# Two-layer encoder step with routed experts: the last rows gathered beside the expert loop end three pairs before the loop does

## The chip, the cores and the metric

The kernel runs on one core of a Trainium2 chip. The metric is the device time of one execution in microseconds (us). The core has five engines with queues of their own: TensorE (PE, matmuls), VectorE (DVE), ScalarE (ACT), GpSimd (POOL) and SyncE (SP), which here only issues transfers. Transfers that SP, ACT and POOL issue share 16 DMA engines.

## The reference

The program takes 512 new frames of one stream and 64 of another (576 tokens, 1024 numbers each) through two layers. Layer 0 mixes tokens with a chunked gMLP, layer 1 with windowed attention; each is followed by the expert step below, and a final norm ends the program. The expert step is where the change lies:

```
def peer_ffn(xn, w_q, sub_keys, exp_u, exp_v):
    q = (xb @ w_q).reshape(blk, PEER_HEADS, 2, D_HALF)
    sc = jnp.einsum('thpd,hpnd->thpn', q, sub_keys)
    ... # per token and head: the best 16 of 16384 experts, idx, with softmax gates
    act = jax.nn.gelu(jnp.einsum('thkd,td->thk', exp_u[idx], xb))
    w = (gate * act)
    return jnp.einsum('thk,thkd->td', w, exp_v[idx])
```

So every token needs, for 8 heads times 16 chosen experts, a dot product with a row of `exp_u` and a weighted sum of rows of `exp_v`.

## The kernel before

The tokens are split in two groups, and each group computes the expert step in its own way, at the same time.

**Dense group ("d", 256 tokens).** All 16384 experts are computed, 256 at a time: 64 "pairs" i = 0..63. For pair i, PE computes scores (`expert_scores`, L725, from `U`), ACT applies GELU (L1106), PE builds a matrix of gates from one-hot factors that DVE makes (`one_hot`, L1634 to L1645, `build`, L712), DVE multiplies gates and scores (`gate_product(l, i)`, L1656, written to `a`), and PE adds the pair's share to the output (`expert_sums`, L738, from `a` and `V`). Scores run 16 pairs (`RING`) and gates 17 pairs (`LEAD`) ahead of the sums. Therefore the last 16 pairs (i = 48..63) have sums and products only. `V` has two buffers: SP loads `V` of pair i + 2 (1 MiB, L451) when sums i are done. `a` has two buffers too: product i waits for sums i - 2. After sums 62, PE adds the residual `hx` with 16 matmuls (L779) and then does sums 63; ACT squares the eight results (L931), PE sums the squares (L541), and DVE turns the sum into the scale of the norm (`variance`, L1406, first instruction of `gathered_to_h` that computes).

**Gathered group ("g", 320 tokens).** Its chosen experts' rows are fetched. One step s (0..319, `NSTEP`) is one indirect DMA on POOL (L1325) that fetches 128 rows of 2048 numbers (1 MiB) into one of six slots (`SLOTS`, tiles `gata`, `gatb`). DVE multiplies and reduces against the tokens (`dot_x`, L1665), ACT makes the weight in two instructions (`weight`, L1112 and L1114), DVE adds the weighted rows to `acc` (`axpy`, L1673). `gathered(l, s)` is dot s and then axpy s - 1. The gather of step s waits for axpy s - 6. Below, a "row step" is one such s.

**Who sets the order.** Each engine runs its own list in order, and the lists are written by hand. The function `steps(l, i)` says which row steps DVE and ACT do in pair i; it takes the numbers from `step0`. On DVE, pair i of the last 16 is: product i + 1, then the row steps of pair i. The row steps thus stand between two products on one engine. Before the loop 57 (layer 0) and 58 (layer 1) row steps are done at fixed places; pairs 0..47 have 4 or 5 each. ACT does its two weight instructions per row step in the same order; in pair 63 it put the last ones between the squares.

PE's own list is not touched by the change, and neither are POOL's and SP's lists; what moves on them follows from waits.

Of the kernel before, what the change touches and what calls it, by code (L numbers as in the profile page):

```python
# [14 lines left out]
DT = D // P  # L15
# [7 lines left out]
NPAIR = NK // 2  # L23
# [14 lines left out]
RING, RING0 = 16, 9  # L38
# [116 lines left out]
def program(nc, xT, ckT, cv, gains, lin, uvd, uvg0, uvg1, skT, wsT, bs, sinks, dist, ident_c, iota_a, scaled_c, rank_c,  # L155
# [5 lines left out]
    with ExitStack() as ctx:  # L161
# [147 lines left out]

        def step0(l, i):  # L310

            n, last = NPAIR - RING, NPAIR
            if i <= n:
                return EARLY[l] + i * BUSY // 2
            rest = NSTEP - EARLY[l] - n * BUSY // 2
            return NSTEP - rest * max(last - i, 0) // (last - n)
# [28 lines left out]
        def steps(l, i):  # L345

            return range(step0(l, i), step0(l, i + 1))
# [28 lines left out]
        def dense_sum(d):  # L376

            return bank[4 + d // 2][:, TD * (d % 2):TD * (d % 2) + TD]
# [546 lines left out]
        def _(act):  # L925
            def square(name, src, dt):

                k, cols = NORM[name], COLS[name[-1]]
                if dt >= 2:
                    act.wait_ge(sq_used, (DT - 1) * k + dt - 1)  # L930
                act.activation(g[:, dt % 2, cols], src, ACT.Square).then_inc(sq_done, 1)  # L931
# [141 lines left out]
            def weights_at(l, place):  # L1073

                for s in early(l, place):
                    weight(l, s)

            def gates_high(l, c):
                b = 4 + c % 2
                act.wait_ge(full[b], BASE[f"gt{l}"][b] + 1)  # L1080
                act.activation(gh[:, TCO[c]:TCO[c] + TCS[c]], bank[b][:, 0:TCS[c]], ACT.Copy,
                               scale=GS).then_inc(gh_done, 1)

            def gate_exp(l, n):

                c = ORDER[n]
                act.wait_ge(sub_done, NTC * l + n + 1)
                act.activation(ex[0:TCS[c]], ex[0:TCS[c]], ACT.Exp).then_inc(exp_done, 1)

            def to_w(l, m):  # L1090

                b, c = 2 + m % 2, m // (TD // TB)
                act.wait_ge(full[b], BASE[f"bld{l}"][b] + m // 2 + 1)
                if m == 0:
                    act.wait_ge(h_out, 16 * (l + 1))
                if c >= 1:
                    act.wait_ge(a_done, NPAIR * l + m - PER + 1)
                act.activation(gate_block(c, m % PER), bank[b][:, :].rearrange("p (t j e) -> p j e t", t=TB, e=2),
                               ACT.Copy, scale=1.0 / GS).then_inc(free[b], 1)

            def gelu(l, i):

                act.wait_ge(full[i % 2], BASE[f"peer{l}"][i % 2] + i // 2 + 1)
                if i >= RING:
                    act.wait_ge(a_done, NPAIR * l + i - RING + 1)
                act.activation(scored(i), bank[i % 2][:, :], ACT.Gelu_apprx_tanh).then_inc(free[i % 2], 1)  # L1106

            def weight(l, s):

                k = s % 8  # L1110
                act.wait_ge(dot_done, NSTEP * l + s + 1)
                act.activation(act8[:, k:k + 1], dot[:, k:k + 1], ACT.Gelu_apprx_tanh).then_inc(act_done, 1)  # L1112
                act.wait_ge(act_done, NSTEP * l + s + 1)
                act.activation(wgt[:, k:k + 1], act8[:, k:k + 1], ACT.Copy, scale=gateg[:, s:s + 1])\  # L1114
                    .then_inc(wgt_done, 1)

            def experts(l):
                n = 0
                for i in range(2 if l else 3, NTC):
                    for k in range(FIRST[l][i] - 1):  # L1120
                        gelu(l, n + k)
                    n += FIRST[l][i]
                    gate_exp(l, i)
                    gelu(l, n - 1)
                    weights_at(l, f"sel{i}")
                    gelu(l, n)
                    n += 1
                for c in DC:
                    gates_high(l, c)
                for i in range(n, RING0 - 1):  # L1130
                    gelu(l, i)
                n = max(n, RING0 - 1)
                weights_at(l, "hot0")
                for m in range(1, LEAD):
                    weights_at(l, f"hot{m}")
                    to_w(l, m - 1)
                    if m % 2 == 1 and n + m // 2 < RING - 1:
                        gelu(l, n + m // 2)
                for i in range(NPAIR):
                    todo = steps(l, i)  # L1140
                    if i == NPAIR - 1:
                        act.wait_ge(full[7], BASE[f"peer{l}"][7] + 1)
                        for dt in range(DT):
                            square(f"n{3 + 2 * l}d", dense_sum(dt), dt)
                            if dt % 2 == 1 and dt // 2 < len(todo):
                                weight(l, todo[dt // 2])
                        todo = todo[DT // 2:]
                    for s in todo[:HEAD]:
                        weight(l, s)
                    if i + LEAD - 1 < NBLD:  # L1150
                        to_w(l, i + LEAD - 1)
                    if i <= NPAIR - RING:
                        gelu(l, i + RING - 1)
                    for s in todo[HEAD:]:
                        weight(l, s)
# [19 lines left out]
            gmlp("d")  # L1175
            selection(0, "d", 2)
            experts(0)

            def squares_of_sums(l):
# [113 lines left out]
            squares_of_h("n4d", "od")  # L1293
            selection(1, "d", 1)
            experts(1)
            squares_of_sums(1)

# [617 lines left out]
```

## Time and profile before

| | |
|---|---|
| median of 3 runs | 3138.45 us (3132.91 to 3144.28) |
| the profiled execution | 3128.67 us, of which the span is 3126.9 us |
| PE matmul busy | 2918.8 us, 93% of the span |
| DVE busy | 2452.2 us, 78% |
| ACT, POOL busy | 793.5 us (25%), 1023.0 us (33%) |
| transfers | 1042.97 MB, mean 334 GB/s |
| mean granted TensorE clock | 0.959 |

A busy PE is not PE at its peak, and a share over the span mixes stages with different limits. So the stage to read is the last 16 pairs of each expert loop: about 1351 to 1529 us in layer 0 and 2937 to 3107 us in layer 1.

### The profile page before, as it was taken

To read this page: it belongs to the slowest core of one execution; us is meant where nothing else is said; L and a number is where in the kernel's file an instruction comes from. 1 tells how busy PE (TensorE), PEld (TensorE's weight loads), DVE (VectorE), ACT (ScalarE), POOL (GpSimd) and SP (SyncE) were. 2 spreads that over 40 slices of the span, in tenths; PEclk is the share of its full clock that TensorE was granted. 3 is DMA by queue.
4 is the path that set the end of the run, shared out by engine and by line. 5 is a ranking of instruction groups with operands and counts; after the bars stand their busy time and mean duration, and the time that the engine had idled before them with its cause. 6 is when DMAs were issued, how large, how long until landed. Compare 5 with 4: busy or idle time off the path is not lost. (4 is left out here: it accounts for less than half of the span.)

```text
span 3126.9 us, 46521 instructions
## 1 busy us (share of the span) xinstructions
PE 2918.8 (93%) x17342; PEld 2556.9 (82%) x17342; DVE 2452.2 (78%) x5319; ACT 793.5 (25%) x2326; POOL 1023.0 (33%) x840
## 2 busy tenths in 40 slices
PE   8898999999999999987888978989999999999977
PEld 7797789888888888876667957879888888888865
DVE  2377899988888888887644777998888888888868
ACT  5332222211121211211354352222111111212112
POOL 5533222322233333333365321222223333333322
PEclk9898999999999999999999979989999999999989
DMA  5327778899999999999622258778999999999997
GB/s 186 102 89 289 306 300 319 349 421 422 421 422 422 416 422 419 418 410 422 230 92 75 93 190 319 283 293 312 422 422 421 422 421 418 421 415 416 413 421 289
DMA packets 159964, 1042.97 MB, mean 334 GB/s; under 512 B 18480, under 2 KB 23920, under 8 KB 44096
## 3 DMA queue, kind: packets, MB, share of 16 engines
q0 software_dynamic: 92160, 671.13, 52.6%
q1 hardware_dynamic: 63648, 357.59, 29.4%
q10 hardware_dynamic: 4000, 12.36, 1.0%
q8 instruction: 74, 1.21, 0.2%
q14 instruction: 82, 0.67, 0.1%
HBM read 1033.28 MB, written 7.86 MB: 333 GB/s over the span
## 5 line engine op out<-in xcount | busy, mean ns | idle before, releaser
L738 PE MATMUL bank<-a,V 128*128 128x256 f32 x4096 | 927.9, 386 | 62.6 <-DVE a L1656 51.2
L725 PE MATMUL bank<-xd,U 128*128 128x256 f32 x4096 | 939.0, 389 | 3.7 <-DMA U<-uvd 3.7
L738 PEld LDWEIGHTS bank<-a,V 128*128 128x128 f32 x4096 | 791.2, 194 | 182.6 <-issue 55.7
L1325 POOL DMA_INDIRECT gata<-uvg,idxg x428 | 496.3, 1159 | 1257.2 <-DVE acc L1673 1197.1
L725 PEld LDWEIGHTS bank<-xd,U 128*128 128x128 f32 x4096 | 789.3, 195 | 112.0 <-DMA U<-uvd 4.7
L1665 DVE CUSTOM_DVE_ANT_0 gata<-gata,xrow 128x1024 f32<-128x1024 f32 x428 | 522.2, 1220 | 222.2 <-DMA gata<-uvg,idxg 220.3
L1112 ACT ACTIVATE act<-dot 128x1 f32<-128x1 f32 x640 | 129.5, 202 | 1672.8 <-DVE dot L1665 1672.7
L1673 DVE SCALAR_TENSOR_TENSOR acc<-gata,wgt,acc 128x1024 f32<-128x1024 f32 x428 | 547.7, 1280 | 2.5 <-ACT wgt L1114 2.3
L1325 POOL DMA_INDIRECT gatb<-uvg,idxg x212 | 251.0, 1184 | 522.6 <-DVE acc L1673 513.1
L1665 DVE CUSTOM_DVE_ANT_0 gatb<-gatb,xrow 128x1024 f32<-128x1024 f32 x212 | 258.7, 1220 | 107.7 <-DMA gatb<-uvg,idxg 106.7
L712 PEld LDWEIGHTS bank<-B,oneA 128*128 128x128 f16 x4096 | 279.3, 150 | 29.9 <-issue 12.8
L712 PE MATMUL bank<-B,oneA 128*128 128x32 f16 x4096 | 283.2, 246 | 14.3 <-DVE oneA L1639 7.2
L1673 DVE SCALAR_TENSOR_TENSOR acc<-gatb,wgt,acc 128x1024 f32<-128x1024 f32 x212 | 271.2, 1279 | 1.9 <-ACT wgt L1114 1.9
L524 PE MATMUL bank<-xd,raw 128*128 128x256 f32 x1088 | 251.0, 388 | 7.5 <-DVE xd L1424 7.1
L524 PEld LDWEIGHTS bank<-xd,raw 128*128 128x128 f32 x1088 | 208.5, 195 | 37.3 <-issue 9.0
L511 PE MATMUL bank<-xh,wh 128*128 128x320 f32 x608 | 200.4, 330 | 29.3 <-POOL xl L418 25.3
L1114 ACT ACTIVATE wgt<-act,gateg 128x1 f32<-128x1 f32 x640 | 188.8, 295 | 20.8
L512 PE MATMUL bank<-xl,wh 128*128 128x320 f32 x608 | 190.9, 314 | 0.0
L513 PE MATMUL bank<-xh,wl 128*128 128x320 f32 x608 | 190.7, 314 | 0.0
L1639 DVE TENSOR_TENSOR oneA<-iotaA,i 128x1024 f16<-128x1024 f16 x256 | 169.9, 703 | 0.0
L511 PEld LDWEIGHTS bank<-xh,wh 128*128 128x128 f32 x608 | 116.9, 192 | 40.4 <-issue 33.7
L1359 POOL TENSOR_TENSOR wl<-raw,wh 128x1024 fp32r<-128x1024 f32 x48 | 115.8, 2414 | 100.6 <-ACT wh L941 100.5
(198 smaller groups left out, 2441.3 us busy)
## 6 DMA issues: line engine op xcount, KB each, us to landing
U<-uvd SPq DMA_DIRECT2D x128, 1024.0 KB
V<-uvd SPq DMA_DIRECT2D x128, 1024.0 KB, 9.0
raw<-lin SPq DMA_DIRECT2D x152, 512.0 KB, 3.6
gata<-uvg,idxg POOLq DMA_INDIRECT x428, 14.7
hsp<-h ACTq DMA_DIRECT2D x2, 2304.0 KB, 14.8
hx<-hsp SPq DMA_DIRECT2D x2, 2304.0 KB, 16.9
gatb<-uvg,idxg POOLq DMA_INDIRECT x212, 14.7
sk_g<-skT ACTq DMA_DIRECT2D x2, 1024.0 KB, 4.9
```

Source lines behind the costliest of these rows:

```text
L511: pe.matmul(out, whi, xh[:, k, :], start=(k == 0), stop=False)
L512: pe.matmul(out, whi, xl[:, k, :], start=False, stop=False)
L513: mm = pe.matmul(out, wlo, xh[:, k, :], start=False, stop=(k == DT - 1))
L524: mm = pe.matmul(bank[s][:, 0:TD], raw[:, s, P * k:P * k + P], x[:, k, :], start=(k == 0), stop=(k == DT - 1))
L712: mm = pe.matmul(bank[2 + s][:, CHUNK * t:CHUNK * (t + 1)], oneA[:, s, t // TG, :, t % TG], B[:, s, part, :, t], start=(t == 0 and part == ...
L725: mm = pe.matmul(bank[s][:, TD * t:TD * t + TD], U[:, s, o:o + P], xd[:, k, :], start=(t == 0 and k == 0), stop=(k == DT - 1), skip_group_ ...
L738: mm = pe.matmul(bank[b][:, TD * (d % 2):TD * (d % 2) + TD], V[:, s, o:o + P], a[:, s, TD * k:TD * k + TD], start=(first and k == 0 and d ...
L1114: act.activation(wgt[:, k:k + 1], act8[:, k:k + 1], ACT.Copy, scale=gateg[:, s:s + 1])\
L1325: pool.indirect_dma_start(row(l, s), None, uvg[l], bass.IndirectOffsetOnAxis(idxg[:, s:s + 1], 0)).then_inc(g_in[s % SLOTS], 16)
L1639: ins = dve.tensor_tensor(oneA[:, s, u], iotaA[:, :, :], i1[:, None, t + TG * u:t + TG * u + TG].broadcast_to([P, P, TG]), ALU.is_equal)
L1665: dve.tensor_tensor_reduce(u, u, xrow[:, min(s // P, 2), :], 1.0, 0.0, ALU.mult, ALU.add, dot[:, s % 8:s % 8 + 1]).then_inc(dot_done, 1)
L1673: dve.scalar_tensor_tensor(out=acc[:, n, :], in0=row(l, s)[:, D:RD], scalar=wgt[:, s % 8:s % 8 + 1], in1=acc[:, n, :], op0=ALU.mult, op1=A ...
```

## The change

`step0(l, i)` gives the first row step of pair i. For the last 16 pairs it divides what remains (47 row steps in layer 0, 46 in layer 1) evenly. Before, it divided by 16, now by 13, so that pairs 61, 62 and 63 get none. Row steps of pairs 48..63:

| | before | after |
|---|---|---|
| layer 0 | 3 in each, 2 in pair 63 | 4 4 3 4 4 3 4 3 4 4 3 4 3 0 0 0 |
| layer 1 | 3 in each, 2 in pairs 55 and 63 | 4 4 3 4 3 4 3 4 3 4 3 4 3 0 0 0 |

In pair 63 ACT no longer has weights to put between the squares, and the code for that goes.

```
@@ -309,7 +309,7 @@
         def step0(l, i):
 
-            n, last = NPAIR - RING, NPAIR
+            n, last = NPAIR - RING, NPAIR - 3
             if i <= n:
                 return EARLY[l] + i * BUSY // 2
             rest = NSTEP - EARLY[l] - n * BUSY // 2
@@ -1142,9 +1142,7 @@
                         act.wait_ge(full[7], BASE[f"peer{l}"][7] + 1)
                         for dt in range(DT):
                             square(f"n{3 + 2 * l}d", dense_sum(dt), dt)
-                            if dt % 2 == 1 and dt // 2 < len(todo):
-                                weight(l, todo[dt // 2])
-                        todo = todo[DT // 2:]
+                            assert not todo
                     for s in todo[:HEAD]:
                         weight(l, s)
```

The change shifts the line numbers behind it by two: L1656, L1665 and L1673 of before are L1654, L1663 and L1671 of after.

DVE's list near the end of layer 1's loop, before, from product 63 (the first row) through the row steps of pair 62 (315 to 317) to those of pair 63:

```order
L1656 TENSOR_TENSOR a_86<-gr_74,Wr_73 128x512
L1665 ISA gata_80,dot_66<-gata_80,xrow_58 128x1024
L1665 ISA dot_66 128x1
L1673 SCALAR_TENSOR_TENSOR acc_77<-gata_80,wgt_68,acc_77 128x1024
L1665 ISA gatb_81,dot_66<-gatb_81,xrow_58 128x1024
L1665 ISA dot_66 128x1
L1673 SCALAR_TENSOR_TENSOR acc_77<-gata_80,wgt_68,acc_77 128x1024
L1665 ISA gatb_81,dot_66<-gatb_81,xrow_58 128x1024
L1665 ISA dot_66 128x1
L1673 SCALAR_TENSOR_TENSOR acc_77<-gatb_81,wgt_68,acc_77 128x1024
L1665 ISA gata_80,dot_66<-gata_80,xrow_58 128x1024
L1665 ISA dot_66 128x1
```

After, from row step 317 of the 320 (its dot is the first row) to the first instruction of the norm:

```order
L1663 ISA gatb_81,dot_66<-gatb_81,xrow_58 128x1024
L1663 ISA dot_66 128x1
L1671 SCALAR_TENSOR_TENSOR acc_77<-gatb_81,wgt_68,acc_77 128x1024
L1663 ISA gata_80,dot_66<-gata_80,xrow_58 128x1024
L1663 ISA dot_66 128x1
L1671 SCALAR_TENSOR_TENSOR acc_77<-gatb_81,wgt_68,acc_77 128x1024
L1663 ISA gata_80,dot_66<-gata_80,xrow_58 128x1024
L1663 ISA dot_66 128x1
L1671 SCALAR_TENSOR_TENSOR acc_77<-gata_80,wgt_68,acc_77 128x1024
L1654 TENSOR_TENSOR a_86<-gr_74,Wr_73 128x512 x2
L1671 SCALAR_TENSOR_TENSOR acc_77<-gata_80,wgt_68,acc_77 128x1024
L1404 TENSOR_SCALAR rstd_61<-bank3 128x256
```

Before, product 63 has five row steps behind it (315 to 319), and product 62 has eight (312 to 319), three of them ahead of product 63. After, products 62 and 63 stand next to each other (the row with x2) behind dot 319 and axpy 318; only the last axpy is behind them.

ACT's list at the same place, before:

```order
L931 ACTIVATE g<-bank 128x256 x2
L1112 ACTIVATE act_67<-dot 128x1
L1114 ACTIVATE wgt<-act_67,gateg 128x1
L931 ACTIVATE g<-bank 128x256 x2
L1112 ACTIVATE act_67<-dot 128x1
L1114 ACTIVATE wgt<-act_67,gateg 128x1
L931 ACTIVATE g<-bank 128x256 x4
L937 ACT_TABLE_LOAD
```

and after:

```order
L1112 ACTIVATE act_67<-dot 128x1
L1114 ACTIVATE wgt<-act_67,gateg 128x1
L1112 ACTIVATE act_67<-dot 128x1
L1114 ACTIVATE wgt<-act_67,gateg 128x1
L931 ACTIVATE g<-bank 128x256 x8
L937 ACT_TABLE_LOAD
```

The two last weights move ahead of the eight squares.

## Rows read from the trace of the kernel before

**Rows 1.** The page: the span in 40 equal slices.
```profile
DMA  5327778899999999999622258778999999999997
GB/s 186 102 89 289 306 300 319 349 421 422 421 422 422 416 422 419 418 410 422 230 92 75 93 190 319 283 293 312 422 422 421 422 421 418 421 415 416 413 421 289
```

**Rows 2.** The page: groups of the row steps, and what transfers take to land.
```profile
L1665 DVE CUSTOM_DVE_ANT_0 gata<-gata,xrow 128x1024 f32<-128x1024 f32 x428 | 522.2, 1220 | 222.2 <-DMA gata<-uvg,idxg 220.3
...
L1673 DVE SCALAR_TENSOR_TENSOR acc<-gata,wgt,acc 128x1024 f32<-128x1024 f32 x428 | 547.7, 1280 | 2.5 <-ACT wgt L1114 2.3
...
V<-uvd SPq DMA_DIRECT2D x128, 1024.0 KB, 9.0
...
gata<-uvg,idxg POOLq DMA_INDIRECT x428, 14.7
...
hx<-hsp SPq DMA_DIRECT2D x2, 2304.0 KB, 16.9
```

**Rows 3.** Windows of layer 1's last 16 pairs (last two columns: DMA share, GB/s).
```profile
2970.00:3000.00 30.00, 22.82 (x93) 18.77 (x92) 22.29 (x30) 4.14 (x17) 9.93 (x9) 0.89 1.01 421
...
3080.00:3090.00 10.00, 7.93 (x29) 6.54 (x29) 7.77 (x11) 1.49 (x6) 3.76 (x3) 0.83 1.02 422
3090.00:3100.00 10.00, 10.00 (x48) 8.81 (x47) 10.00 (x14) 1.99 (x8) 1.14 (x1) 1.00 0.72 290
```

**Rows 4.** Timeline of DVE, layer 1: products 49, 62, 63; dot 319; norm.
```profile
2947.30 0.68 DVE L1656 TENSOR_TENSOR a<-gr,Wr 128x512 f32<-128x512 f32 x1
...
3081.45 0.69 DVE L1656 TENSOR_TENSOR a<-gr,Wr 128x512 f32<-128x512 f32 x1
...
3091.40 0.68 DVE L1656 TENSOR_TENSOR a<-gr,Wr 128x512 f32<-128x512 f32 x1
...
3101.38 1.22 DVE L1665 CUSTOM_DVE_ANT_0 gata<-gata,xrow 128x1024 f32<-128x1024 f32 x1
...
3106.77 0.43 DVE L1406 TENSOR_SCALAR rstd<-bank 128x256 f32<-128x256 f32 x1 [1.47 <-PE bank L541]
```

**Rows 5.** Timeline of PE, layer 1: sums 61, sums 62, residual, sums 63, norm.
```profile
3071.38 8.83 PE L738 MATMUL bank<-a,V 128*128 128x256 f32 x32 [3.73 <-DVE a L1656]
3082.29 8.83 PE L738 MATMUL bank<-a,V 128*128 128x256 f32 x32 [2.07 <-DVE a L1656]
3090.95 3.62 PE L779 MATMUL bank<-hx,ident 128*128 128x256 f32 x16
3094.41 7.07 PE L738 MATMUL bank<-a,V 128*128 128x256 f32 x32
3102.04 4.62 PE L541 MATMUL bank<-g,ones 128*128 128x256 f32 x16 [0.56 <-ACT g L931]
```

**Rows 6.** Timeline of DVE, layer 0: products 49, 62, 63; dot 319; norm.
```profile
1359.78 0.69 DVE L1656 TENSOR_TENSOR a<-gr,Wr 128x512 f32<-128x512 f32 x1
...
1497.63 0.69 DVE L1656 TENSOR_TENSOR a<-gr,Wr 128x512 f32<-128x512 f32 x1
...
1506.61 0.68 DVE L1656 TENSOR_TENSOR a<-gr,Wr 128x512 f32<-128x512 f32 x1
...
1522.65 1.23 DVE L1665 CUSTOM_DVE_ANT_0 gata<-gata,xrow 128x1024 f32<-128x1024 f32 x1 [0.47 <-DMA gata<-uvg,idxg]
...
1528.67 0.42 DVE L1406 TENSOR_SCALAR rstd<-bank 128x256 f32<-128x256 f32 x1 [2.19 <-PE bank L541]
```

**Rows 7.** Timeline of PE, layer 0: sums 62 and sums 63.
```profile
1498.46 7.14 PE L738 MATMUL bank<-a,V 128*128 128x256 f32 x32 [1.11 <-DVE a L1656]
...
1508.90 7.07 PE L738 MATMUL bank<-a,V 128*128 128x256 f32 x32
```

**Rows 8.** Timeline of SP and a window, end of layer 0's loop.
```profile
1474.87 22.84 SPq L451 DMA_DIRECT2D V<-uvd  x3
1497.88 1.96 SPq L435 DMA_DIRECT2D raw<-lin  x4
...
1510.00:1520.00 10.00, 7.07 (x32) 5.60 (x30) 6.03 (x8) 1.82 (x7) 0.00 (x0) 0.97 0.89 364
```

More of the change, by code:

```diff
@@ L310, in step0 @@
         def step0(l, i):
-            n, last = NPAIR - RING, NPAIR
+            n, last = NPAIR - RING, NPAIR - 3
             if i <= n:
@@ L1144, in experts @@
                             square(f"n{3 + 2 * l}d", dense_sum(dt), dt)
-                            if dt % 2 == 1 and dt // 2 < len(todo):
-                                weight(l, todo[dt // 2])
-                        todo = todo[DT // 2:]
+                        assert not todo
                     for s in todo[:HEAD]:
```

## The prediction

> **What bounds the kernel now.** I read the 40 slices of the page first, then the windows of the last 16 pairs, then the timelines of DVE and PE at the end of both loops. The slices show long stretches at 410 to 422 GB/s with the DMA engines full [rows 1]. In the last 16 pairs the reader is to see the same: DMA share 1.01, 421 GB/s, while PE is busy for 22.8 of 30 us and DVE for 22.3 [rows 3]. So here neither engine is full, and the transfers set the pace: in layer 1 from product 49 to product 62 pass 3081.45 - 2947.30 = 134.15 us [rows 4]. In that time DVE does the row steps of pairs 48 to 60, which are 38 (12 pairs of 3 and one of 2). With 13 loads of V (V50 to V62) and the one load of hx (2.25 MiB [rows 2]) that is 53.25 MiB, 2.52 us per MiB or 416 GB/s. DVE's own work on a row step is shorter, 1.22 + 1.28 us less an overlap of about 0.1 [rows 2], some 2.4 us.
>
> The end is a different matter, and there the order on DVE counts. PE waits for product 61 (3.73 us) and for product 62 (2.07 us); then it runs sums 62, the residual, sums 63 and the norm's sums without a hole to speak of [rows 5]. From the start of product 62 to the norm's first DVE instruction at 3106.77 is one unbroken chain of 25.3 us [rows 4]. Eight row steps (312 to 319: three of pair 61, three of pair 62, two of pair 63) stand behind product 62 on DVE and run beside that chain. They end at 3101.38 + 1.22 and two axpys, about 3105, before it does. In layer 0 the chain would end alone at about 1497.63 + 24 us = 1522; the norm starts only at 1528.67 [rows 6], because dot 319 begins at 1522.65 and ACT's last weights stand between the squares. There the rows decide, by some 7 us. They are late because SP issues four tiles of the next weights (raw, 2 MiB together) right behind V63 at 1497.88 [rows 8].
>
> **The change, part by part.**
>
> Removed and added instructions: none on DVE, PE, POOL or SP; ACT has the same 640 pairs of weight instructions. Everything is order, and bytes stay the same.
>
> *Where the rows end up.* Product 62 had eight row steps behind it and now stands behind all of them, but for axpy 319. So it comes when all 320 gathers have landed. I work that time out in two ways for layer 1.
> (a) By pace: from product 49 the remaining 46 row steps, 13 loads of V and hx are 61.25 MiB. Some 3 MiB come off: at the end of the measured stretch six gathers were issued and about half moved, and now none is left. 58.25 x 2.52 = 146.8 us, which gives 2947.3 + 146.8 = 3094.1.
> (b) By the end of all transfers: the window 3090 to 3100 moves 290 GB/s, 2.9 MB, which at 421 GB/s last until 3096.9 [rows 3]. Of this, V63 now goes behind the rows (it waits for sums 61), 2.5 us; the last row has landed at 3094.4, a straggling landing may cost 0 to 3 us, and dot 319 and axpy 318 take 2.4: 3096.8 to 3099.8.
> I take 3097.5, nearer to (b), which rests on the end itself. Product 62 therefore moves by 3097.5 - 3081.45 = +16.0 us.
> The same for layer 0: (a) 1359.78 + (47 + 13 + 2.25 - 3) x 2.52 = 1509.1; (b) window 1510 to 1520 with 364 GB/s ends at about 1518.6 [rows 8], less V63 and the four raw tiles (3 MiB, 7.6 us) is 1511.0, plus 2.4 and a straggling landing of 0 to 4 (dot 319 began 4 us after 1518.6): 1513.4 to 1517.4. I take 1514.5.
>
> *What follows it.* The chain behind product 62 has nothing beside it that can be taken off: product 0.7, sums 62 7.1 to 8.8, residual 3.5, sums 63 7.1, squares and their sums 5.3 [rows 5, 7], which is 23.6 to 25.3 us. ACT's two weights (about 0.5 us each) go from between the squares. In layer 1 that gives nothing: PE's 16 norm matmuls last 4.62 us back to back [rows 5]. In layer 0 they no longer wait for a late row, and this gain is in the numbers below.
> Layer 1: 3097.5 + 25.3 = 3122.8 against 3106.77, +16.0 us.
> Layer 0: 1514.5 + 24.5 = 1539.0 against 1528.67, +10.3 us.
> What comes behind the norm (transposes of acc, the next layer, the stores) is unchanged and moves as a block; axpy 319 waits for product 63 and so for sums 61, but is done long before PE asks for acc.
>
> *What is costed at nothing, and its cover.* The pairs 48 to 60 get longer (from 134.15 / 13 = 10.3 us to about 11.5 us each), so PE waits more in each. That is off the path, since PE needs 7.1 to 8.8 us a pair. V63 is issued when sums 61 end. Product 61 is three row steps ahead of product 62, 8 to 10 us, so sums 61 end at about 3096 to 3099, and V63 lands 9.0 us later [rows 2], at 3105 to 3108. Sums 63 ask for it at 3097.5 + 0.8 + 8.8 + 3.5 = 3110.6. The cover is some 3 us. In layer 0 the raw tiles are issued behind V63: 3 MiB in 7.6 us from about 1514, done by 1524, asked for at 1527. If this cover is gone the price is the lateness itself, 1 to 4 us per layer.
>
> *The sum:* 10.3 + 16.0 = +26.3, with rounding +27 us. Against the profiled execution 3128.67 + 27 = 3155.7 us. That execution lies 9.8 us under the median of the runs, so against the median it is 3138.45 + 27 = **3165 us**, 0.86% slower.
>
> **A rule beside the row.** The row shows 421 GB/s for whole stretches [rows 3]. The Trainium skill, "DMA: Bandwidth & Descriptors", section "Where 436 GB/s comes from", gives about 358 GB/s per core as the bound for transfers from HBM and 435 GB/s as that of the fabric. At 358 GB/s (an estimate from that page) 58.25 MiB would take 170.6 us and product 62 would come at 3118 rather than near 3095; the trace is above this bound by 63 GB/s, and the measurement decides.
>
> **The rivals.**
>
> 1. *Faster: the gathers had room, and denser rows fill it.* If the pace of before was set by the thin list (3 rows per pair, each slot refilled only after its axpy) and not by bytes, then 3.5 rows per pair run at DVE's floor: 46 x 2.4 + 13 x 0.6 = 118 us, product 62 at 3065.5 in layer 1, 16 us earlier than before; in layer 0 1359.8 + 120.6 + 24.5 = 1504.9, 24 us earlier. That gives 3138.45 - 40 = 3098 us. For it: DVE is idle for a quarter of the stretch, waiting for gathers. Against it: DMA share 1.01 [rows 3]. It decides when a MiB takes under 134.15 / 58.25 = 2.30 us (455 GB/s) in layer 1, which no window shows. Chance 0.03. The skill's page named above has the fabric's 435 GB/s as ceiling, so by its rule this rival is shut as well.
>
> 2. *About the same.* The landing of rows gets shorter where fewer loads of V compete, and the pace comes to 2.40 us per MiB (437 GB/s): product 62 at 2947.3 + 139.8 = 3087.1 (+5.7) and at 1502.0 in layer 0, whose norm is then at 1526.5 (-2.2). In sum +3.5, 3142 us. For it speaks that single slices and windows reach 422 to 424; against it that none reaches 437. Chance 0.08.
>
> 3. *Slower still.* V63 or the clock adds to the tail. Product 62 comes as late as 3100.5 and 1518, V63 is 2 to 4 us late, and sums 62 and 63 run partly at 1.2 GHz: sums 62 took 8.83 us after an idle stretch of 2.07 us and 7.14 after one of 1.11 [rows 5, 7], with a granted clock down to 0.83 in that window [rows 3]. Longer idle time in front could raise both sums to about 2 x 7.1 = 14.2 us, up to 5 and 7 us more. Sum +38 to +50, 3176 to 3188 us. Against it: the last three rows drain at 2.4 to 3.2 us, so that product 62 comes about when sums 61 end, and PE has no wait there. Chance 0.07. The skill, "TensorE: Matmul & The Clock Gate", section "HAM oscillation — how this bites in real kernels", says that an engine that waits for transfers in every round begins every round at the low clock; by it, sums 62 would be at 8.8 rather than 7.1 us, which is the value that I took for layer 1.
>
> That the change doesn't do what it says is excluded by the lists of the engines: the two products stand side by side at the end.
>
> **How the numbers follow.** My own case has 0.82. Its bounds: product 62 from 3094 to 3100 with a chain of 23.6 to 25.3 us, +10.8 to +19; layer 0 from 1509 to 1518 likewise, +4 to +14.6. Together +15 to +34, 3153 to 3172 us. To leave out no more than 2 in 10 the range is stretched a little towards rivals 2 and 3: 3150 to 3176. A measurement of this kernel tells about 0.3% (9.4 us) from no change, so rival 2 and the thin lower end are "same": 0.08 for same, 0.04 for faster, 0.88 for slower.
>
> **What would show it.** In the profile of the changed kernel: in the stretch of pairs 48 to 60 a DMA share near 1.0 and about 420 GB/s (if lower, the six slots became the limit and rows take longer). Product 62 at 147 to 153 us behind product 49 in layer 1. The two products back to back with the second waiting for sums 61; then sums 62, residual and sums 63 with idle DMA engines and a DVE that has nothing to do. DVE's wait in front of the norm grows from 1.47 us to some 20 us. No wait of sums 63 for V. The prediction is wrong if product 62 comes at or before the time it had (the rows were not bound by bytes), or if the time behind it is shorter than 23 us.

## The result, and the profile after

| | before | after |
|---|---|---|
| median | 3135.68 us (3127.08 to 3144.28, 4 runs) | 3163.05 us (3161.42 to 3170.66, 4 runs) |
| ratio | | 1.0092, 95% interval 1.0058 to 1.0126 |
| profiled execution, its span | 3128.67, 3126.9 us | 3170.66, 3168.9 us |

The kernel became slower: by 27.4 us, 0.87%, between the medians, and by 28.9 us, 0.92%, between the means, which is the ratio of the table. The forecast was 3165 us (3150 to 3176), +27 us.

The page of after, the span in 40 slices, beside [rows 1]:

```profile
DMA  5237788899999999999422258778999999999995
GB/s 184 82 99 292 280 316 312 352 421 421 422 422 422 420 419 416 416 409 419 170 90 72 92 188 315 297 282 328 422 422 422 422 422 416 422 416 418 411 417 198
```

The long stretches are as full as they were. What differs is the end of each loop (a slice is 79 us wide): 170 GB/s where it was 230 in the slice of layer 0's end, 198 where it was 289 in the last one. So more of both ends passes with idle DMA engines.

Timeline of DVE of after, layer 1: product 49, dot 318, dot 319 and axpy 318, products 62 and 63, the last axpy, the norm. It answers to [rows 4].

```profile
2970.75 0.69 DVE L1654 TENSOR_TENSOR a<-gr,Wr 128x512 f32<-128x512 f32 x1
...
3119.37 1.22 DVE L1663 CUSTOM_DVE_ANT_0 gata<-gata,xrow 128x1024 f32<-128x1024 f32 x1 [1.14 <-DMA gata<-uvg,idxg]
...
3122.75 1.23 DVE L1663 CUSTOM_DVE_ANT_0 gata<-gata,xrow 128x1024 f32<-128x1024 f32 x1 [0.95 <-DMA gata<-uvg,idxg]
...
3123.90 1.28 DVE L1671 SCALAR_TENSOR_TENSOR acc<-gata,wgt,acc 128x1024 f32<-128x1024 f32 x1
3125.10 0.69 DVE L1654 TENSOR_TENSOR a<-gr,Wr 128x512 f32<-128x512 f32 x1
3125.95 0.69 DVE L1654 TENSOR_TENSOR a<-gr,Wr 128x512 f32<-128x512 f32 x1 [0.17 <-PE bank L738]
3126.57 1.28 DVE L1671 SCALAR_TENSOR_TENSOR acc<-gata,wgt,acc 128x1024 f32<-128x1024 f32 x1
3148.74 0.43 DVE L1404 TENSOR_SCALAR rstd<-bank 128x256 f32<-128x256 f32 x1 [20.89 <-PE bank L541]
```

The reader is to see the two products side by side behind the last row, and then DVE idle for 20.89 us (before: 1.47), waiting for PE's norm sums.

Timeline of PE of after, the same end: sums 61 and 62 as one entry, the residual, sums 63, the norm. It answers to [rows 5].

```profile
3116.03 17.05 PE L738 MATMUL bank<-a,V 128*128 128x256 f32 x64 [3.59 <-DVE a L1654]
3132.92 3.62 PE L779 MATMUL bank<-hx,ident 128*128 128x256 f32 x16
3136.37 7.07 PE L738 MATMUL bank<-a,V 128*128 128x256 f32 x32
3144.01 4.62 PE L541 MATMUL bank<-g,ones 128*128 128x256 f32 x16 [0.56 <-ACT g L931]
```

Sums 62 follow sums 61 with a hole of only 0.12 us (PE is busy for 5.88 of the 6.00 us in the window 3120 to 3126 below). Product 62 ran from 3125.10 to 3125.79, and sums 61 ended at about 3125.8. What follows is PE's work, with ACT's squares between sums 63 and the norm's sums.

Windows of after (the last two columns are the DMA share and GB/s; the one before them is the granted clock as a share of 2.4 GHz):

```profile
3100.00:3110.00 10.00, 7.90 (x29) 6.34 (x29) 7.72 (x10) 1.49 (x6) 4.40 (x4) 0.83 1.02 424
3110.00:3120.00 10.00, 6.41 (x21) 5.00 (x20) 8.44 (x11) 1.49 (x6) 0.00 (x0) 0.73 0.87 363
3120.00:3126.00 6.00, 5.88 (x25) 4.77 (x23) 4.88 (x8) 1.00 (x4) 0.00 (x0) 0.88 0.03 11
3126.00:3130.00 4.00, 4.00 (x19) 3.54 (x20) 1.84 (x2) 0.00 (x0) 0.00 (x0) 1.00 0.79 256
3130.00:3149.00 19.00, 18.31 (x85) 14.62 (x84) 0.27 (x1) 4.07 (x9) 0.00 (x0) 1.00 0.01 2
```

The DMA engines are full until about 3118, then carry V63 from 3126, then nothing while PE finishes.

Two stretches carry the comparison: P, from product 49 to product 62 (both read off DVE's timeline), and T, from product 62 to the norm's first DVE instruction. Us:

| profile | layer 0 P | T | P+T | layer 1 P | T | P+T |
|---|---|---|---|---|---|---|
| before | 137.85 | 31.04 | 168.89 | 134.15 | 25.32 | 159.47 |
| after | 157.84 | 23.64 | 181.48 | 154.35 | 23.64 | 177.99 |

That is +12.6 and +18.5, 31.1 us of the 42.0 by which this profiled span is longer. Another 8.0 are there before the change acts (product 49 of layer 0 at 1367.78 us against 1359.78), and 2.9 lie between the two loops. The second profile of each kernel, below, shows that the 8.0 are not the change's.

### The profile page after: what moved, and what is told of

It reads as the page before. It is cut to its first block and busy times, and to the rows that moved or that the text cites. A ratio compares the mean times of both kernels' runs of the same rounds, so it can differ in the third digit from the quotient of the medians.

```text
span 3168.9 us, 46521 instructions
## 1 busy us (share of the span) xinstructions
PE 2939.6 (93%) x17342; PEld 2572.0 (81%) x17342; DVE 2455.9 (77%) x5319; ACT 794.9 (25%) x2326; POOL 1043.4 (33%) x840
## 5 line engine op out<-in xcount | busy, mean ns | idle before, releaser
L738 PE MATMUL bank<-a,V 128*128 128x256 f32 x4096 | 941.4, 390 | 88.8 <-DVE a L1654 83.9
L738 PEld LDWEIGHTS bank<-a,V 128*128 128x128 f32 x4096 | 800.7, 196 | 212.8 <-issue 92.7
L1323 POOL DMA_INDIRECT gata<-uvg,idxg x428 | 513.6, 1200 | 1229.5 <-DVE acc L1671 1169.9
L1663 DVE CUSTOM_DVE_ANT_0 gata<-gata,xrow 128x1024 f32<-128x1024 f32 x428 | 522.3, 1221 | 220.4 <-DMA gata<-uvg,idxg 217.8
L1671 DVE SCALAR_TENSOR_TENSOR acc<-gata,wgt,acc 128x1024 f32<-128x1024 f32 x428 | 548.1, 1281 | 0.9 <-ACT wgt L1114 0.9
L1663 DVE CUSTOM_DVE_ANT_0 gatb<-gatb,xrow 128x1024 f32<-128x1024 f32 x212 | 258.8, 1221 | 102.0 <-DMA gatb<-uvg,idxg 100.2
L1671 DVE SCALAR_TENSOR_TENSOR acc<-gatb,wgt,acc 128x1024 f32<-128x1024 f32 x212 | 271.3, 1280 | 0.0
## 6 DMA issues: line engine op xcount, KB each, us to landing
gata<-uvg,idxg POOLq DMA_INDIRECT x428, 14.7
gatb<-uvg,idxg POOLq DMA_INDIRECT x212, 14.7
```

Source lines behind the costliest of these rows:

```text
L738: mm = pe.matmul(bank[b][:, TD * (d % 2):TD * (d % 2) + TD], V[:, s, o:o + P], a[:, s, TD * k:TD * k + TD], start=(first and k == 0 and d ...
L1323: pool.indirect_dma_start(row(l, s), None, uvg[l], bass.IndirectOffsetOnAxis(idxg[:, s:s + 1], 0)).then_inc(g_in[s % SLOTS], 16)
L1663: dve.tensor_tensor_reduce(u, u, xrow[:, min(s // P, 2), :], 1.0, 0.0, ALU.mult, ALU.add, dot[:, s % 8:s % 8 + 1]).then_inc(dot_done, 1)
L1671: dve.scalar_tensor_tensor(out=acc[:, n, :], in0=row(l, s)[:, D:RD], scalar=wgt[:, s % 8:s % 8 + 1], in1=acc[:, n, :], op0=ALU.mult, op1=A ...
```

## The experiments

In all of them P and T are read as above. "Behind product 62" is the number of row steps that DVE still has to do after it (8 before, 0 after). Single executions of the kernel before lie anywhere from 3126.4 to 3144.0 us (23 runs), so for a kernel that ran once the stretches count, and its total is given only as it is.

### The changed kernel once more

No edit.

> The changed kernel once more, unaltered, for a second profile. My theory (product 62 waits for all gathers, and the tail behind it lies bare): from product 49 to the norm's first DVE instruction 178 to 184 us in layer 0 and 175 to 181 us in layer 1, as in the first profile (181.5 and 178.0; before: 168.9 and 159.5). The 8 us by which the first profile already lagged at product 49 of layer 0 are the run's own (a stretch of low clock at 100 to 200 us) and should not come again in the same size. Rival: the lag at product 49 belongs to the change; then it is 8 us again.

Layer 0: P 156.52, T 23.64, together 180.16. Layer 1: 154.02 and 23.63, together 177.65. Product 49 of layer 0 stood at 1360.85 us, and the total was 3163.44 us. So the 8 us belong to that one execution. The windows of 100 to 200 us show where they come from: the first profile of after has a granted clock of 0.88 there and 551 matmuls done, this one 0.97 and 600.

One thing differs at the end. Rows of DVE, layer 1: dot 318, then products 62 and 63 as one entry.

```profile
3113.09 1.23 DVE L1663 CUSTOM_DVE_ANT_0 gata<-gata,xrow 128x1024 f32<-128x1024 f32 x1 [1.91 <-DMA gata<-uvg,idxg]
...
3117.89 1.29 DVE L1654 TENSOR_TENSOR a<-gr,Wr 128x512 f32<-128x512 f32 x2
```

Dot 318 waits for its gather, but dot 319 follows at 3115.54 without a wait, and product 62 comes 4.8 us behind dot 318: two row steps of DVE. Layer 0 is the same in both profiles of after. Only in layer 1 of the first profile did dot 319 wait as well (0.95 us above).

### The kernel before once more

> The kernel before once more, unaltered, for a second profile, so that the spread of its stage times is known. Expected: product 49 to norm 168.9 us in layer 0 and 159.5 us in layer 1, each within 1.5 us; product 49 of layer 0 at either of the two levels seen so far (1360 or 1368 us).

Layer 0: P 137.75, T 31.02, together 168.77. Layer 1: 135.43 and 25.14, together 160.57, product 49 of layer 0 at 1360.49 us. P+T repeats within 1.1 us here and within 1.3 us for after; P alone repeats within 1.3 us. Between this and the repeat of after the change costs 11.4 us in layer 0 and 17.1 in layer 1, 28.5 us, close to the 27.4 of the medians.

### 14 pairs: three row steps behind product 62

```
-            n, last = NPAIR - RING, NPAIR
+            n, last = NPAIR - RING, NPAIR - 2
```
(on the kernel before, ACT's code as it was)

> The remaining row steps over 14 pairs: 3 row steps stand behind product 62 instead of 0 (after) or 8 (before). My theory: each row step put ahead of product 62 moves it by about 2.4 us, so product 49 to norm is 171 to 174 us in layer 1 and 173 to 176 in layer 0, about +17 us on the kernel before. Rival (what costs is the missing work beside the last products, as soon as any pair is empty, or denser rows at the start): the same as with 13 pairs, +27 us.

Layer 0: P 148.94, T 23.64, together 172.58 (+3.7). Layer 1: P 144.32, T 27.23, together 171.55 (+12.1). Total 3155.84 us (before, run beside it, 3137.34) in an execution with product 49 of layer 0 at 1368.92, so again with the 8 us that are not the change's. Layer 1 falls into the expected 171 to 174, layer 0 half a us below its 173 to 176. The rival's fixed cost would have given 180 and 178. In layer 1 T is 3.6 us longer than with 13 pairs: V62's load was issued at 3100.03, when sums 60 ended, and landed 9.4 us later, so sums 62 waited 2.48 us for it. They then took 8.86 us and not 7.14.

### 15 pairs: six row steps behind product 62

```
-            n, last = NPAIR - RING, NPAIR
+            n, last = NPAIR - RING, NPAIR - 1
```

> The remaining row steps over 15 pairs: 6 stand behind product 62. My theory: layer 1 +4 to +5 us (163 to 165 us from product 49 to norm); layer 0 unchanged within 2 us (about 169), since there the rows end last and the tail has 7 us of room. Total +3 to +6 us. Rival (fixed cost of an empty pair): about +9 us or more in each layer.

Layer 0: P 142.17, T 24.96, together 167.13 (-1.8). Layer 1: P 139.02, T 23.63, together 162.65 (+3.2). Layer 1 came 0.4 us below its range, and both stages together at +1.4 us where +3 to +6 were expected. The total of this one execution, 3133.07 us (before, run beside it, 3137.34), is too coarse to settle that. The 9 us per layer that the rival asked for an empty pair did not come. In layer 0, where PE's chain had room in T, P grows by 4.3 us and the end does not move later.

P in layer 1 over the row steps moved ahead of product 62 (0, 2, 5, 8): 134.2, 139.0, 144.3, 154.4 us. That is 2.5 us each over all eight, but not evenly: 2.4 each for the first two, 1.8 for the next three, 3.3 for the last three, which also make product 62 wait for the last gather.

### Fewer bytes, the order of after

This kernel leaves out 31/32 of each V from pair 50 on.

```
                 def v_load(i, s):
-                    sp.dma_start(V[:, s, :], uvd[bass.ds(i * 2 + (2 * NPAIR * l + 1), 1), :, :].rearrange(
+                    n = 64 if i >= NPAIR - RING + 2 else RD
+                    sp.dma_start(V[:, s, 0:n], uvd[bass.ds(i * 2 + (2 * NPAIR * l + 1), 1), :, 0:n].rearrange(
```

> The changed kernel with the loads of V for pairs 50 to 63 cut to 64 of 2048 columns (their sums use stale numbers; matmuls and all waits stay). It takes some 13 MiB out of the stretch. My theory (bytes set the pace of the rows): product 49 to product 62 in layer 1 falls from 154 us to 118 to 126 us, where DVE's own 2.4 us per row step becomes the floor; the kernel gets about 55 to 65 us shorter, with the tail behind product 62 unchanged at 23 to 25 us. Rival (the six slots and the waits around them set the pace, not bytes): it stays above 145 us.

Layer 0: P 126.67, T 24.60. Layer 1: P 123.67, T 24.60, together 148.27. Total 3115.31 us, 55.4 less than the first profiled execution of after, which had the same lag at product 49 (1369.10 here). Windows of layer 1:

```profile
2950.00:3000.00 50.00, 41.08 (x179) 34.68 (x179) 49.18 (x64) 9.81 (x39) 30.55 (x21) 0.97 1.01 404
3000.00:3050.00 50.00, 37.57 (x155) 31.07 (x154) 44.02 (x59) 8.47 (x35) 25.70 (x18) 0.93 1.02 418
```

DVE is busy for 49.18 of 50 us at first, its floor. The DMA engines are full in both windows as well (share 1.01 and 1.02), now almost with rows alone. So bytes do set the pace of after: 12.6 MiB less (13 loads, 1/32 of each left) made P 30.7 us shorter, 2.44 us per MiB. The six slots were not what held the rows at the pace of after.

### Fewer bytes, the order of before

The same edit on the kernel before.

> The kernel before with the loads of V for pairs 50 to 63 cut to 64 of 2048 columns (their sums use stale numbers). My theory: without these bytes rows run at 2.7 us each, as with the order of after (123.7 us for 46), so product 49 to 62 is 100 to 106 us for 38; and the order still costs: product 49 to norm is 125 to 132 us against 148.3 with the order of after, a difference of 16 to 23 us in layer 1 although the DMA engines are no longer full. Rival: the tail is bare only because V63 and the last gathers crowd each other; then the two orders come within 5 us.

Layer 0: P 108.27, T 28.81, together 137.08. Layer 1: P 103.46, T 23.63, together 127.09, total 3068.02 us. Against the order of after with the same bytes (151.27 and 148.27) the order costs 14.2 and 21.2 us. So the loss is not a crowd of V63 and the last gathers: with the V loads nearly gone, it is as large as it was. One part of the expectation failed: the DMA engines are still full (share 1.02, 417 GB/s in the window 2950 to 3022), since the rows now come faster. The pair therefore shows that V63's crowding is not needed for the loss; it does not show the loss without full DMA engines.

### ACT's part alone

```
                     if i == NPAIR - 1:
+                        for s in todo:
+                            weight(l, s)
                         act.wait_ge(full[7], BASE[f"peer{l}"][7] + 1)
                         for dt in range(DT):
                             square(...)
-                            if dt % 2 == 1 and dt // 2 < len(todo):
-                                weight(l, todo[dt // 2])
-                        todo = todo[DT // 2:]
+                        todo = todo[:0]
```

> The kernel before with one part of the change alone: ACT makes the weights of pair 63's row steps before the eight squares instead of between them. My theory: this part is worth nothing; product 49 to norm stays 168.9 us (layer 0) and 159.5 us (layer 1) within 2 us. Rival: weights between the squares held the norm back in layer 0; then layer 0 gains 1 to 2 us, or, since the first squares now wait for dot 319 too, it loses about 2.

Layer 0: P+T 171.04 (+2.2), layer 1: 162.14 (+2.7), total 3144.46 us. My "worth nothing" fell: with the rows where they were, the interleaved order is worth 2 to 3 us in each layer (T alone grows by 2.6 and 2.7 us), since weights that wait for dot 319 hold all eight squares. That is the last branch of the rival. Two rows of PE's timeline in layer 1 of this kernel:

```profile
3105.82 7.07 PE L738 MATMUL bank<-a,V 128*128 128x256 f32 x32
3116.69 5.75 PE L541 MATMUL bank<-g,ones 128*128 128x256 f32 x16 [3.80 <-ACT g L931]
```

PE waits 3.80 us for the first squares, where it had waited 0.56 [rows 5]. In the changed kernel this costs nothing, because there no row step is left by then.

### The raw tiles later

```
+            sp.wait_ge(ax_done, NSTEP - 1)
             for name in LOADS[6:]:
                 linear(name)
             experts(1)
```
(on the kernel before)

> The kernel before, with SP waiting for axpy 318 of layer 0 before it issues the next four weight tiles (raw, 2 MiB) and all behind them. My theory: these bytes are what makes the last rows of layer 0 late; product 49 to norm falls in layer 0 from 168.9 to 162 to 165 us, layer 1 stays at 159.5, the total is 4 to 7 us less. Rival (a straggling landing at the end of any burst): layer 0 stays within 1.5 us of 168.9.

Layer 0: P 136.50, T 24.51, together 161.01 (-7.9). Layer 1: 158.55 (-0.9). Total 3135.32 us with product 49 of layer 0 at 1370.06. Layer 0 ends 1 us earlier than the 162 to 165 expected, while this one execution is 2.2 us shorter than the 3137.47 of before run beside it, not 4 to 7. Then the same kernel ran 12 times:

> The late raw tiles alone, timed. My theory: 7 to 9 us less than before by layer 0's stage (161.0 against 168.9), layer 1 as before: ratio about 0.9975. Rival: the gain in the stage is given back behind it, where the next layer's first tiles land later; then the ratio is 1.

Median 3128.46 us (12 runs) against 3133.28 (23 runs), ratio 0.9981, interval 0.9968 to 0.9994. That is 4.8 us less, where 7 to 9 were expected; the interval allows some 2 to 10. Its profile has P+T 161.66 and 158.54. The 7.2 us are not given back behind it: from layer 0's norm to the end pass 1598.1 us, against 1598.2 and 1601.8 in the two profiles of before. SP and DVE of that profile, layer 0:

```profile
1520.93 1.75 SPq L435 DMA_DIRECT2D raw<-lin  x4
```
```profile
1518.37 1.23 DVE L1666 CUSTOM_DVE_ANT_0 gata<-gata,xrow 128x1024 f32<-128x1024 f32 x1
...
1522.91 0.42 DVE L1407 TENSOR_SCALAR rstd<-bank 128x256 f32<-128x256 f32 x1 [0.71 <-PE bank L542]
```

With the four tiles issued at 1520.9 and not at 1497.9 [rows 8], dot 319 comes without a wait at 1518.37, and T, 24.49 us, is within 0.9 us of PE's bare chain. This shows that the raw tiles made layer 0's last rows late.

### Eleven row steps behind product 62

```
-            rest = NSTEP - EARLY[l] - n * BUSY // 2
-            return NSTEP - rest * max(last - i, 0) // (last - n)
+            tail = 11
+            if i >= NPAIR - 3:
+                return NSTEP - tail + tail * (i - NPAIR + 3) // 3
+            first = EARLY[l] + n * BUSY // 2
+            return first + (NSTEP - tail - first) * (i - n) // (NPAIR - 3 - n)
```
(on the kernel before)

> The opposite of the change: 11 row steps stand behind product 62 (3, 4, 4 in pairs 61 to 63) instead of 8. My theory: product 62 comes 7 us earlier (126 to 130 us behind product 49 in layer 1), but now the rows end last, so that the norm in layer 1 stays within 2 us of 159.5, and layer 0 within 2 us of 168.9. Rival (each row step moved behind product 62 gains its 2.4 us): both layers gain 5 to 7 us.

Layer 0: P 130.52, T 36.33, together 166.85 (-2.0). Layer 1: P 124.72, T 32.97, together 157.69 (-1.8). Total 3134.70 us. P falls by 9.4 us in layer 1, more than the 4 to 8 us expected, and 7.7 of them come back in T. DVE of layer 1:

```profile
3109.22 2.67 DVE L1676 SCALAR_TENSOR_TENSOR acc<-gata,wgt,acc 128x1024 f32<-128x1024 f32 x2
3111.81 0.42 DVE L1409 TENSOR_SCALAR rstd<-bank 128x256 f32<-128x256 f32 x1
```

The norm starts when the last axpy ends; no wait stands ahead of it. The rows are now the last to end, as the theory has it.

### Both: eleven behind product 62 and late raw tiles

> Both edits that gained: 11 row steps behind product 62, and SP waiting for axpy 318 of layer 0 before it issues the raw tiles. My theory: the rows' landing is then the only bound at the end of both loops; product 49 to norm 157 to 160 us in layer 0 (before 168.9, the late raw tiles alone 161.0) and 157 to 158.5 in layer 1 (before 159.5, 11 behind alone 157.7). Total 9 to 13 us less than before, ratio about 0.9965. Rival: the two gains are one and the same in layer 0 (161) and the total is no better than with the late raw tiles alone.

Median 3126.50 us (12 runs) against 3133.28 (23 runs), ratio 0.998, interval 0.9966 to 0.9994. P+T 161.82 in layer 0 and 157.70 in layer 1. The total is 6.8 us less than before, where 9 to 13 were expected, and layer 0 missed its 157 to 160. Layer 0 is no better than with the late raw tiles alone, as the rival had it: there product 62 is early, DVE does the last rows back to back at 2.4 us each, and their end decides. Both versions are faster than before by a fifth of a per cent, clear of the interval; between the two no difference was measured.

## Why the prediction was right

**The step that decides.** Product 62 comes after all the gathers, and the chain behind it lies bare. The lists said so, the profile shows it (20.89 us of idle DVE), and the series 8, 6, 3, 0 row steps behind product 62 moves P step by step; eleven behind it move P the other way. That V63 crowding the last gathers is not the cause is shown by the pair with small V: still 21 us between the orders in layer 1.

**Bytes set the pace.** Rival 1 (room for denser rows) and rival 2 (2.40 us per MiB, 437 GB/s) are out: in layer 1 of after the DMA engines ran at 418 GB/s, share 1.01, from product 49 to 3118, against 421 over P of before. In those 147.25 us they moved 58.7 MiB, close to the 58.25 of reading (a). The small-V kernel shows the same from the other side.

**Sizes that were off, and cancelled.** Layer 1's product 62 was put 150.2 us behind product 49 and came at 154.35 and 154.02. That is outside the 147 to 153 named as a sign, and later than even the 3100.5 of rival 3 (153.2 behind product 49). The byte count was right: at their full rate the DMA engines would have run dry at about 3118.7, 148 us behind product 49, where the forecast had 147.1 (in layer 0 152 and 151 us, forecast 151.2). The term that was too small is what follows. It was put at 3.1 us (dot 319, axpy 318 and 0.7 for a straggling landing; 3.5 in layer 0) and measured some 5.5 to 6.5 us in both layers of both profiles. In all four, dot 318 already waits for its gather, until about 0.6 to 1.6 us after that time, so two row steps, 4.8 us, stand ahead of product 62 and not one of 2.4. In one of the four dot 319 waits as well, for 0.95 us.

The chain behind product 62 was put at 25.3 us in layer 1 and took 23.64, its lower bound. The difference is sums 62, for which 8.8 us were taken: they waited 0.1 to 1.2 us in the two profiles and ran at the high clock in 7.14 us. In sum +16.0 was forecast in layer 1 and 18.5 and 17.1 measured. In layer 0 P was put at 154.7 and was 157.84 and 156.52, T 24.5 against 23.64: +10.3 forecast, 12.6 and 11.4 measured.

So the mechanism was right, but that 27 meets 27.4 so closely is luck. The stages moved by 31.1 and 28.5 us where 26.3 were forecast, and the medians are of four runs each. Against the 23 later runs of before (median 3133.28 us) after is 29.8 us slower; the forecast of 3165 stood on three runs whose median was 5 us above that.

**The covers.** V63 cost nothing: its load was issued when sums 61 ended, at 3125.8, and landed 6.4 us later, before sums 63 at 3136.37, which show no wait. Of rival 3 only the late product 62 came: no wait for V there, and the clock in the last window is 1.00. The condition I gave against it (product 62 comes about when sums 61 end) held.

**The missed part.** ACT's weights ahead of the squares were costed at nothing. For the changed kernel nothing speaks against that (PE waits 0.56 us ahead of the norm's sums, as before); taken alone they cost 2 to 3 us per layer.

**Layer 0's 7 us of room** was put down to the raw tiles. Moving them gave 7.9 and 7.2 us, so this is shown. It also fits why the change cost 5.7 to 5.9 us less in layer 0: P grew by 20.0 us there and by 20.2 in layer 1, but T fell by 7.4 us against 1.7. The changed kernel with late raw tiles was not run.

## What to carry to other kernels

When two streams of work end together on an in-order engine, look at which one has the longer chain behind its last item on that engine. Here a product has 24 us of PE work behind it and a row step 4 us, so products go ahead of rows, up to the point where the rows end last (eleven behind product 62 gained only 2 us); emptying the last pairs of rows put all rows ahead of the products, and bared the long chain. A list that is evenly spread to the end can be right just because it leaves cheap work to lie beside the expensive end; when transfers set the pace, count the bytes that must have landed before the last product, and move every transfer that nobody needs yet behind them.

## What the runs showed of the hardware beside it

The end of a burst of transfers is not sharp. In layer 1 of after the traffic falls from 421 GB/s (3115 to 3118) to 197, 74 and then 22 GB/s (3118 to 3119, 3119 to 3120, 3120 to 3123); in the last of these the DMA share is 0.05, on average less than one of 16 engines. Gather 319 was issued at 3108.41 and released its dot at 3122.75, 14.3 us later, no longer than the median landing of 14.7 us [rows 2]. In layer 0 of before it is alike: 18 GB/s from 1520 to 1523, with dot 319 at 1522.65. In the other three loop ends of after dot 319 did not wait. Why the last megabyte trickles was not tested.

Product 49 of layer 0 comes at 1359.8 to 1361.3 us in six of the 13 profiles, at 1367.8 to 1370.1 in five and at 1365.0 and 1365.1 in two, and the kernel does not decide which: the two profiles of after lie in different groups, and so do the two of the kernel with late raw tiles. The granted clock in the window of 100 to 200 us goes with it: 0.95 to 0.97 in the first group, 0.88 to 0.90 in the others. What makes the clock fall there in some executions stays open.
